# Grouped attention's scores as three products of rounded halves instead of one fp32 product

## The chip, the cores and the metric

The kernel runs on one core of a Trainium2 chip. The metric is the device time of one execution in microseconds (us); a version's time is the median of three runs. The core's engines that matter here are TensorE (PE: matrix products and transposes, written to PSUM banks of 128 x 512 fp32), ScalarE (ACT), VectorE (DVE), and the queue of SyncE (SP), which starts most of the loads.

## The reference, cut to what matters

The reference is two transformer-like blocks of two layers each over 512 tokens of width 2048, all in fp32. The change touches one of the three attention branches of the first block, branch A (grouped attention, 8 query heads over 2 key heads, 128 wide):

```
proj = rms_norm(x, g_pre) @ w_in            # 2048 -> 5952, split into a_q, a_k, a_v, a_g, ...
qa = rope_axial(rms_norm(a_q), row, col)    # 512 tokens x 8 heads x 128
ka = rope_axial(rms_norm(a_k), row, col)    # 512 tokens x 2 heads x 128
s  = einsum('bqkgd,bskd->bkgqs', qa, ka) * 128 ** -0.5      # all 512 keys, no mask
p  = softmax(s)
o_a = (p @ va) * silu(a_g)
...
y = concat(o_a, o_b, o_c) @ w_out
x = x + rms_norm(y, g_post)
```

## The kernel before, in words

**Panels.** All large products (`panel`, L619 to L643) run as "panels" of 512 output columns. Each weight tile arrives in `stage`; ScalarE writes its rounded copy `whi` (type F32R), VectorE writes the rest `wlo = stage - whi`, and TensorE adds up three products of rounded operands: `hi_x*lo_w`, `hi_x*hi_w`, `lo_x*hi_w` (L635, L636, L637). The activations are split the same way into `act_hi` and `act_lo`. The product of the two low parts is left out.

**Branch A.** After panel 8 of each of the first block's two layers, the branch starts. Queries and keys lie in `zone` with tokens on the partitions. A "turn job" (`job`, L668) transposes one head's four 128 x 128 tiles into one of two banks `JOB`; VectorE copies the bank to `zone` (`take_job`, L1473) as `kT_a` (2 heads) or `qT_a` (ring of 4 heads). Two key jobs and the first query job come first, and then one query job per head, one head ahead of its use.

Scores go by "units": unit i is head i // 4 and query tile i % 4, 32 units per layer. TensorE's order for unit i is: `score(i)`, one fp32 product of 128 x 128 with 128 x 512 (L680); `turn(i-2)`, four transposes of the probabilities (L689); `pv(i-3)`, four fp32 products with the values (L698). At i = 0, 4, 8, ... the next head's query job (L668) stands in front.

- VectorE for unit i: `row_max(i)`, a maximum over 512 scores (L1489) and its product with a scale (L1491); then `finish(i-3)`, a reciprocal and two products (L1501, L1503, L1506). At a head's first unit, the copy of the next head's queries (L1473) stands in front.
- ScalarE for unit i: `take_turn(i-2)`, copying turned probabilities out of their bank (L1152); then `exp(i)` (L1144).

Each engine executes its own list in order, and semaphores tie them. `score(i)` waits for `exp(i-2)`, since it writes the bank that this one reads; `turn(i)` waits for `exp(i)`; `pv(i)` waits for `take_turn(i)` and for `finish(i-2)`. A query job waits until the job two before it has left its bank (`job_ev`), and a head's first score waits for `job_ev` of its queries. No scheduler is at work: the order is that of the loops.

Of the kernel before, what the change touches and what calls it, by code (L numbers as in the profile page):

```python
# [8 lines left out]
F32 = mybir.dt.float32  # L9
F32R = mybir.dt.float32r  # L10
I32 = mybir.dt.int32
ALU = mybir.AluOpType
ACT = mybir.ActivationFunctionType
AX = mybir.AxisListType

P = 128
SEQ = 512
TT = SEQ // P
# [10 lines left out]
HD = 128  # L29
A_H, A_KV, B_H, C_H = 8, 2, 4, 4  # L30
# [104 lines left out]
def build(nc, io, only_first=False):  # L135


    with ExitStack() as ctx:
# [26 lines left out]
        zone_at = place[0]  # L165
# [45 lines left out]
        def view(first, *shape, of=zone):  # L211

            size = int(np.prod(shape))
            names = "abcd"[:len(shape)]
            v = of[:, first:first + size]
            if len(shape) == 1:
                return v
            return v.rearrange(f"p ({' '.join(names)}) -> p {' '.join(names)}",
                               **{n: s for n, s in zip(names, shape)})

        xs = view(0, TT, DM)
        probs = view(PP, 4, SEQ)
        probsT = view(PP + 2048, 4, SEQ)
        tanh_tmp = view(ZT, 2, PW)
# [22 lines left out]
        def count(name, per1, per2=None, credit=0):  # L247
            return Count(sem(name), (per1, per1 if per2 is None else per2), credit)
# [18 lines left out]
        J1, J2 = 46, 29  # L267
        job_done = count("job_done", J1, J2)
        job_ev = count("job_ev", J1, J2, credit=2)
        score_done = count("score_done", UNITS, PAIRS)  # L270
        max_done = count("max_done", UNITS, 2 * PAIRS)
        exp_done = count("exp_done", UNITS, PAIRS, credit=2)
# [62 lines left out]
        qT_c, kT_c, v_c = view(ZT, C_H, SEQ), view(ZK, C_H, SEQ), view(ZV, TT, PW)  # L335
        g_c = view(ZQ, C_H, GM, GRID_W)
        q_a, kv_a = view(ZQ, TT, A_H * HD), view(ZV, TT, 2 * A_KV * HD)
        qT_a, kT_a = view(ZT, 4, SEQ), view(ZK, A_KV, SEQ)

        cq_b, ckv_b = view(ZQ, TT, B_Q), view(ZV, TT, B_CKV_W)  # L340
        wuq, wukv = view(PP, 4, 768), view(ZK, 2, 1024)
# [15 lines left out]
        def tok(t):  # L357
            return slice(t * P, (t + 1) * P)
# [2 lines left out]
            return [(qT_c[:, h, tok(t)], kT_c[:, h, :])]  # L361

        def scores_a(h, t):
            return [(qT_a[:, h % 4, tok(t)], kT_a[:, h // 4, :])]

        def scores_b(h, t):
            return [(qnT[:, h, tok(t)], knT[:, h, :]), (qpT[0:B_ROPE, h, tok(t)], kpT[0:B_ROPE, :])]
# [10 lines left out]
        def turn_job(srcs, width, dst, scale=1.0):  # L378
            return ("turn", srcs, width, dst, scale)

        def mm_job(groups, n, dst, scale=1.0):
# [3 lines left out]
                  for h in range(C_H)] + \  # L385
                 [turn_job([view(PP, TT, PW)[:, t, h * HD:(h + 1) * HD] for t in range(TT)], P, qT_c[:, h, :], -SC_C)
                  for h in range(C_H)]
        JOBS_AK = [turn_job([kv_a[:, t, h * HD:(h + 1) * HD] for t in range(TT)], P, kT_a[:, h, :]) for h in range(A_KV)]
        JOBS_AQ = [turn_job([q_a[:, t, h * HD:(h + 1) * HD] for t in range(TT)], P, qT_a[:, h % 4, :]) for h in range(A_H)]
        B_QC, B_KC = KC, KC + 4  # L390
        wuq_h = wuq.rearrange("p k (h e) -> p k h e", h=B_H)
        wukv_h = wukv.rearrange("p k (h e) -> p k h e", h=B_H)
# [624 lines left out]
        def _(act):  # L1017
# [129 lines left out]
            def take_turn(blk, l, br, i):  # L1147
                u = br["first"] + i
                act.wait_ge(turn_done.sem, turn_done.at(blk, l, u + 1))
                act.wait_ge(pv_done.sem, pv_done.at(blk, l, u + 1 - 4))  # L1150
                w = P * len(range(TT))
                act.activation(probsT[:, u % 4, 0:w], TURN[u % 2][:, 0:w], ACT.Copy).then_inc(pt_done.sem, 1)  # L1152

            def attention(blk, l, br):
                n = 4 * br["heads"]
                for i in range(n + 2):
                    if i >= 2:
                        take_turn(blk, l, br, i - 2)
                    if i < n:
                        exp(blk, l, br, i)  # L1160

            def pair_exp(l, i):
                w = P * len(keys_of(i % 4))
# [39 lines left out]
            with act.Fori(0, 2) as l:  # L1203
                for j in range(LEAD):
                    split_hi(0, l, 0, j)
                act.wait_ge(job_ev.sem, job_ev.at(0, l, 1))
                in_panel(l, 0, take_copy(lambda t, p: view(0, TT, PW)[:, t, :]), turned=turned_then_saved(l),
                         between=squares_between(l))
                in_panel(l, 1, take_copy(lambda t, p: view(2048, TT, PW)[:, t, :]), row=0)
                in_panel(l, 2, take_copy(lambda t, p: v_c[:, t, :]), row=1)  # L1210
                in_panel(l, 3, take_tanh(), row=2)
                attention(0, l, BR_C)
                with act.Fori(4, 6) as p:
                    in_panel(l, p, take_copy(lambda t, p: zone[:, bass.ds(ZQ + t * 1024 + (p - 4) * PW, PW)]), row=p - 1)
                in_panel(l, 6, take_copy(lambda t, p: kv_a[:, t, :]), row=5)
                in_panel(l, 7, take_tanh(), row=6)
                in_panel(l, 8, take_tanh())
                attention(0, l, BR_A)
                in_panel(l, 9, take_copy(lambda t, p: cq_b[:, t, :]), next_width=B_CKV_W)
                in_panel(l, 10, take_copy(lambda t, p: ckv_b[:, t, :], B_CKV_W), width=B_CKV_W, row=7)  # L1220
                in_panel(l, 11, take_tanh(), row=8)
                attention(0, l, BR_B)
                out_panel(0, l, NIN, True, turned=turned_hi(0, l, KC, 0.5))
                out_panel(0, l, NIN + 1, True)
                out_panel(0, l, NIN + 2, True, row=9)
                out_panel(0, l, NP - 1, False, row=10)
                mod_row_out(l, NIN - 1)
# [71 lines left out]
            with act.Fori(0, 2) as l:  # L1299
# [21 lines left out]
                high = turned_hi(1, l, KC, 0.5)  # L1321
# [17 lines left out]
        def _(dve):  # L1339
# [125 lines left out]
            def take_job(blk, l, n, jb):  # L1465
# [8 lines left out]
                else:  # L1474
                    dve.tensor_scalar(dst, src, scale, None, ALU.mult).then_inc(job_ev.sem, 1)

            def row_max(blk, l, br, i):
                u = br["first"] + i
                h, t = i // 4, i % 4
                dve.wait_ge(score_done.sem, score_done.at(blk, l, u + 1))  # L1480


                s, m, nm = SCORE[u % 2][:, :], nmx[:, u % 4, 0:1], nmx[:, u % 4, 1:2]
                if br["name"] == "C":
                    bias = g_c[:, h, 6 - 2 * t:14 - 2 * t, :].rearrange("p m k -> p (m k)")
                    apart(dve)
                    dve.tensor_tensor_reduce(s, s, bias, 1.0, 3.0e38, ALU.add, ALU.min, nm).then_inc(max_done.sem, 1)
                elif br["name"] == "A":
                    dve.tensor_reduce(m, s, AX.X, ALU.max, negate=True).then_inc(dve_link.next(), 1)  # L1489
                    dve.wait_ge(dve_link.sem, dve_link.now(blk, l))  # L1490
                    dve.tensor_tensor(nm, m, rsq[:, t, h:h + 1], ALU.mult).then_inc(max_done.sem, 1)  # L1491
                else:
                    dve.tensor_reduce(nm, s, AX.X, ALU.max, negate=True).then_inc(max_done.sem, 1)  # L1493
# [178 lines left out]
            for l in range(2):  # L1672
# [24 lines left out]
                panel(0, l, 6, take_copy(lambda t, p: kv_a[:, t, :]), mod=6)  # L1697
                panel(0, l, 7, take_gate(lambda p: 0, lambda p: 1), between=a_between1(l))
                panel(0, l, 8, take_gate(lambda p: PW, lambda p: 2), between=a_between2(l))
                j0 = BR_A["j0"]  # L1700
                for n, jb in enumerate(JOBS_AK + JOBS_AQ[0:1]):
                    take_job(0, l, j0 + n, jb)

                def next_queries(h):
                    if h + 1 < A_H:
                        take_job(0, l, j0 + 3 + h, JOBS_AQ[h + 1])
                attention(0, l, BR_A, next_queries)
                panel(0, l, 9, take_copy(lambda t, p: cq_b[:, t, :]), next_width=B_CKV_W, mod=7)
                panel(0, l, 10, take_copy(lambda t, p: ckv_b[:, t, :], B_CKV_W), width=B_CKV_W, mod=8)
# [465 lines left out]
```

## Time and profile before

| what | value |
|---|---|
| median of 3 runs | 3671.71 us (3661.34 to 3674.33) |
| the profiled execution's own time, core 0 | 3671.2 us, its span from first to last instruction 3671.2 us |
| PE busy | 3515.5 us, 96% |
| DVE busy | 1834.7 us, 50% |
| ACT busy | 1113.0 us, 30% |
| mean granted clock of TensorE | 0.979 |
| branch A, layer 0 (first transpose to next panel) | 481.17 to 558.92 us |

An engine's busy time is a share of the whole span. Matmuls are pipelined and the printed length of one is modelled, so the pace of TensorE is read from the distance between starts. A printed fp32 product of 512 columns has two records, and an fp32 product of 128 columns also has two.

### The profile page before, as it was taken

What the parts mean: (1) busy time and instruction counts of PE and PEld (TensorE: products, weight loads), DVE (VectorE), ACT (ScalarE), POOL (GpSimd) and SP (SyncE); (2) the same over time, 40 slices, a digit from 0 to 9 for tenths busy, and PEclk for the clock granted to TensorE, in tenths of its full rate; (3) what the DMA queues carried; (4) which work ended last, traced back from release to release, by engine and by line L of the source; (5) the groups of instructions that cost most, each with busy time, mean ns of one, the idle gap of its engine ahead of it and who ended that gap; (6) DMA issues with size and microseconds to landing.
All of it is one profiled execution on the core that took longest, in us unless ns stands there. A gap on an engine that the chain in (4) does not pass through costs nothing.

```text
span 3671.2 us, 49811 instructions
## 1 busy us (share of the span) xinstructions
PE 3515.5 (96%) x17037; PEld 2800.2 (76%) x17037; DVE 1834.7 (50%) x3318; ACT 1113.0 (30%) x1784; POOL 151.9 (4%) x218
## 2 busy tenths in 40 slices
PE   7999999999999999999997999999997999999998
PEld 6878878668787887875876887787786888778786
DVE  5555765445665556654456323546625332626543
ACT  3232242132322323422223223432323222522431
POOL 1101001001110100000010000000000000000000
PEclk9999999999999999999998999999998999999999
DMA  7636316025664452330644332231333333033142
GB/s 267 209 94 198 112 30 204 29 103 179 203 210 148 156 159 60 115 118 1 207 149 136 92 100 66 61 103 36 134 100 113 98 97 97 18 95 92 53 149 97
DMA packets 183839, 430.27 MB, mean 117 GB/s; under 512 B 18166, under 2 KB 25777, under 8 KB 177240
## 3 DMA queue, kind: packets, MB, share of 16 engines
q1 hardware_dynamic: 151144, 298.11, 25.4%
q0 software_dynamic: 28992, 104.43, 9.2%
q10 hardware_dynamic: 3504, 25.22, 1.7%
q8 instruction: 108, 1.77, 0.2%
q14 instruction: 91, 0.75, 0.1%
HBM read 406.61 MB, written 24.75 MB: 117 GB/s over the span
## 4 chain that ended last, share of the span: by engine, by line
PE 89%; DVE 6%; DMA 2%; issue 2%; ACT 1%; DVEq 0%; ACTq 0%; SPq 0%; POOLq 0%
PE bank L635 23%; PE bank L637 23%; PE bank L636 23%; PE bank L680 4%; PE bank L698 3%; PE bank L672 2%; PE bank L689 2%; PE bank L659 1%; PE bank L835 1%; PE bank L813 1%; DMA wmod<-in_w_mod 1%; PE bank L824 1%; PE bank L668 1%; PE bank L889 1%; PE bank L876 1%
## 5 line engine op out<-in xcount | busy, mean ns | idle before, releaser
L635 PE MATMUL bank<-wlo,act_hi 128*128 128x512 f32 (+1 forms) x3968 | 1552.3, 391 | 9.2 <-DVE zone L1394 4.6
L637 PE MATMUL bank<-whi,act_lo 128*128 128x512 f32 (+1 forms) x3968 | 1538.5, 388 | 0.0
L636 PE MATMUL bank<-whi,act_hi 128*128 128x512 f32 (+1 forms) x3968 | 1538.2, 388 | 0.0
L1347 DVE TENSOR_TENSOR wlo<-stage,whi 128x1024 fp32r<-128x1024 f32 (+1 forms) x496 | 598.1, 1210 | 810.6 <-ACT whi L1023 809.0
L1023 ACT ACTIVATE whi<-stage 128x1024 fp32r<-128x1024 f32 (+1 forms) x496 | 514.8, 1048 | 1469.0 <-PE bank L637 816.8
L635 PEld LDWEIGHTS bank<-wlo,act_hi 128*128 128x128 f32 x3968 | 747.3, 188 | 181.1 <-issue 21.2
L637 PEld LDWEIGHTS bank<-whi,act_lo 128*128 128x128 f32 x3968 | 747.1, 188 | 152.7
L636 PEld LDWEIGHTS bank<-whi,act_hi 128*128 128x128 f32 x3968 | 747.7, 188 | 146.5
L1362 DVE SCALAR_TENSOR_TENSOR macc<-wmod,csil,macc 128x512 f32<-128x512 f32 x360 | 269.8, 749 | 101.5 <-DMA wmod<-in_w_mod 72.2
L2130 POOL DMA_DIRECT2D wmod<-in_w_mod x192 | 136.6, 712 | 1749.6 <-DVE macc L1362 1728.6
L1152 ACT ACTIVATE zone<-bank 128x512 f32<-128x512 f32 x128 | 76.4, 597 | 137.2 <-PE bank L689 137.0
L689 PEld LDWEIGHTS bank<-ident,zone 128*128 128x128 f32 x512 | 61.4, 141 | 67.6 <-issue 61.7
L1523 DVE TENSOR_TENSOR Y<-bank,zone 128x512 f32<-128x512 f32 (+1 forms) x64 | 43.2, 691 | 123.2 <-ACT mprod L1191 65.6
L680 PE MATMUL bank<-zone 128*128 128x512 f32 x192 | 98.7, 599 | 5.7 <-ACT zone L1144 3.9
L698 PE MATMUL bank<-zone 128*128 128x128 f32 x768 | 101.0, 275 | 0.0
L1412 DVE SCALAR_TENSOR_TENSOR Y<-zone,bank 128x512 f32<-128x512 f32 (+1 forms) x64 | 43.6, 687 | 104.9 <-ACT zone L1073 102.9
L698 PEld LDWEIGHTS bank<-zone 128*128 128x128 f32 x768 | 93.2, 192 | 0.0
L659 PE MATMUL bank<-ident,Y 128*128 128x128 f32 x384 | 59.6, 289 | 27.5 <-DMA Y<-in_x 14.1
L1144 ACT ACTIVATE zone<-bank,nmx 128x512 f32<-128x512 f32 x64 | 43.8, 685 | 125.0 <-DVE nmx L1493 104.1
L659 PEld LDWEIGHTS bank<-ident,Y 128*128 128x128 f32 x384 | 49.1, 149 | 39.7 <-issue 21.5
L689 PE MATMUL bank<-ident,zone 128*128 128x128 f32 x512 | 78.4, 276 | 0.0
L680 PE MATMUL bank<-late 64*128 64x512 f32 (+1 forms) x128 | 66.8, 622 | 1.6 <-DVE late L1473 1.6
(222 smaller groups left out, 2465.3 us busy)
## 6 DMA issues: line engine op xcount, KB each, us to landing
stage<-in_w_in SPq DMA_DIRECT2D x352, 512.0 KB, 3.7
wmod<-in_w_mod POOLq DMA_DIRECT2D x192, 512.0 KB, 4.4
stage<-in_w_out SPq DMA_DIRECT2D x128, 512.0 KB, 3.9
out<-Y ACTq DMA_DIRECT2D x20, 1024.0 KB, 5.5
zone<-out SPq DMA_DIRECT2D x4, 4096.0 KB, 15.3
stage<-in_w_in SPq DMA_DIRECT2D x16, 320.0 KB, 3.8
Y<-in_x ACTq DMA_DIRECT2D x4, 1024.0 KB, 9.1
rpb_tiles<-rpb_pad POOLq DMA_DIRECT2D x16, 224.0 KB, 7.6
```

What stands on the lines that cost most here:

```text
L635: pe.matmul(out, hi_x, lo_w, start=(k == 0), stop=False)
L636: pe.matmul(out, hi_x, hi_w, start=False, stop=False)
L637: mm = pe.matmul(out, lo_x, hi_w, start=False, stop=(k == KC - 1))
L659: tr = pe.transpose(XP[k % 4][:, tok(t)], src[:, t, tok(k)], ident[:, :])
L680: mm = pe.matmul(SCORE[u % 2][:, 0:P * len(range(TT))], lhs, rhs, start=(r == 0), stop=(r == len(parts) - 1))
L689: mm = pe.transpose(TURN[u % 2][:, tok(kt)], probs[:, u % 4, tok(kt)], ident[:, :])
L698: mm = pe.matmul(OUTB[u % 2][:, 0:HD], probsT[:, u % 4, tok(n)], br["v"](i // 4, kt), start=(n == 0), stop=(n == len(tiles) - 1))
L1023: act.activation(whi[:, j % RH, :, 0:width], stage[:, j % RS, :, 0:width], ACT.Copy)\
L1152: act.activation(probsT[:, u % 4, 0:w], TURN[u % 2][:, 0:w], ACT.Copy).then_inc(pt_done.sem, 1)
L1347: dve.tensor_tensor(wlo[:, j % RH, :, 0:width], stage[:, j % RS, :, 0:width], whi[:, j % RH, :, 0:width].bitcast(F32), ALU.subtract).then_ ...
L1362: dve.scalar_tensor_tensor(out=macc[:, :], in0=wmod[:, i % 2, k % 2, :], scalar=csil[:, k:k + 1], in1=macc[:, :], op0=ALU.mult, op1=ALU.ad ...
L2130: pool.dma_start(wmod[:, i % 2, :, :], src.rearrange("o (a p) n -> p (o a) n", p=P))\
```

## The change

Queries and keys of branch A are kept as two F32R tiles, high and low. `split_a` holds 4 x 2 x 512 columns, in the place of the old `qT_a` and `kT_a` and of what was free behind them; the ring of queries goes from 4 heads to 2. A job's bank is now read twice: ScalarE copies it with rounding to the high part (`split_high`), and VectorE, once that is there, subtracts the high part from the bank (`split_low`). `job_ev` comes from `split_low`. A score is three F32R products into the same bank instead of one fp32 product; the product of the two low parts is left out.

```diff
+        split_a = sb("split_a", [P, 4, 2, SEQ], F32R, at=zone_at + 4 * ZT)
+        a_hi = count("a_hi", A_KV + A_H, 0)
...
-        qT_a, kT_a = view(ZT, 4, SEQ), view(ZK, A_KV, SEQ)
+        qT_hl, kT_hl = split_a[:, 0:2, :, :], split_a[:, 2:4, :, :]
...
         def scores_a(h, t):
-            return [(qT_a[:, h % 4, tok(t)], kT_a[:, h // 4, :])]
+            q, k = qT_hl[:, h % 2, :, :], kT_hl[:, h // 4, :, :]
+            return [(q[:, 1, tok(t)], k[:, 0, :]), (q[:, 0, tok(t)], k[:, 1, :]), (q[:, 0, tok(t)], k[:, 0, :])]
...
+        SPLIT_A = [kT_hl[:, h, :, :] for h in range(A_KV)] + [qT_hl[:, h % 2, :, :] for h in range(A_H)]
...                                                     # ScalarE
-            def attention(blk, l, br):
+            def attention(blk, l, br, early=None):
                 n = 4 * br["heads"]
                 for i in range(n + 2):
                     if i >= 2:
                         take_turn(blk, l, br, i - 2)
+                    if early and i % 4 == 0 and i < n:
+                        early(i // 4)
                     if i < n:
                         exp(blk, l, br, i)
+
+            def split_high(l, m):
+                n = BR_A["j0"] + m
+                act.wait_ge(job_done.sem, job_done.at(0, l, n + 1))
+                act.activation(SPLIT_A[m][:, 0, :], JOB[n % 2][:, :], ACT.Copy).then_inc(a_hi.sem, 1)
...
-                attention(0, l, BR_A)
+                for m in range(A_KV + 1):
+                    split_high(l, m)
+                attention(0, l, BR_A, lambda h: split_high(l, A_KV + 1 + h) if h + 1 < A_H else None)
...                                                     # VectorE
+            def split_low(l, m):
+                n = BR_A["j0"] + m
+                dve.wait_ge(a_hi.sem, a_hi.at(0, l, m + 1))
+                high, low = SPLIT_A[m][:, 0, :], SPLIT_A[m][:, 1, :]
+                dve.tensor_tensor(low, JOB[n % 2][:, :], high.bitcast(F32), ALU.subtract).then_inc(job_ev.sem, 1)
...
-                j0 = BR_A["j0"]
-                for n, jb in enumerate(JOBS_AK + JOBS_AQ[0:1]):
-                    take_job(0, l, j0 + n, jb)
+                for m in range(A_KV + 1):
+                    split_low(l, m)
 
                 def next_queries(h):
                     if h + 1 < A_H:
-                        take_job(0, l, j0 + 3 + h, JOBS_AQ[h + 1])
+                        split_low(l, A_KV + 1 + h)
```

TensorE's list at the start of head 1 (unit 4) before: a query job, then `score(4)` into bank4, `turn(2)` into bank2, `pv(1)` into bank7.

```order
L668 MATMUL bank1<-ident_60,zone_56 128x128 x4
L767 REGISTER_ALU
L677 REGISTER_ALU
L680 MATMUL bank4<-zone_56 128x512
L689 MATMUL bank2<-ident_60,zone_56 128x128 x4
L698 MATMUL bank7<-zone_56 128x128 x4
```

The same place in the changed kernel (its lines stand 4 further down).

```order
L672 MATMUL bank1<-ident_60,zone_56 128x128 x4
L771 REGISTER_ALU
L681 REGISTER_ALU
L684 MATMUL bank4<-split_a_93 128x512 x3
L693 MATMUL bank2<-ident_60,zone_56 128x128 x4
L702 MATMUL bank7<-zone_56 128x128 x4
```

Nothing moved on TensorE: one product became three in the same place.

ScalarE's list there before: `exp(3)`, `take_turn(2)` from bank2, `exp(4)`, `take_turn(3)`, `exp(5)`.

```order
L1144 ACTIVATE zone_56,sm_74<-bank5,nmx_73,rsq_72 128x512
L1149 REGISTER_ALU
L1152 ACTIVATE zone_56<-bank2 128x512
L1144 ACTIVATE zone_56,sm_74<-bank4,nmx_73,rsq_72 128x512
L1149 REGISTER_ALU
L1152 ACTIVATE zone_56<-bank3 128x512
L1144 ACTIVATE zone_56,sm_74<-bank5,nmx_73,rsq_72 128x512
```

And in the changed kernel:

```order
L1148 ACTIVATE zone_56,sm_74<-bank5,nmx_73,rsq_72 128x512
L1153 REGISTER_ALU
L1156 ACTIVATE zone_56<-bank2 128x512
L1171 REGISTER_ALU
L1172 ACTIVATE split_a_93<-bank1 128x512
L1148 ACTIVATE zone_56,sm_74<-bank4,nmx_73,rsq_72 128x512
L1153 REGISTER_ALU
L1156 ACTIVATE zone_56<-bank3 128x512
L1148 ACTIVATE zone_56,sm_74<-bank5,nmx_73,rsq_72 128x512
```

The split (L1172) is new; it stands behind the copy of the turned probabilities of two units before and ahead of the head's first exp. On VectorE the copy of the queries, L1473, is replaced one for one by the subtraction, L1496, ahead of the head's first row maximum:

```order
L1496 TENSOR_TENSOR split_a_93<-bank1,split_a_93 128x512
L1510 TENSOR_REDUCE nmx_73<-bank4 128x1
L1512 TENSOR_TENSOR nmx_73<-nmx_73,rsq_72 128x1
L1522 RECIPROCAL ri_75<-sm_74 128x1
L1524 TENSOR_TENSOR ri_75<-ri_75,xr_64 128x1
```

Its number of instructions is unchanged; what it waits for is now ScalarE and no longer TensorE.

## Rows read from the trace of the kernel before

**Rows 1.** The page: busy time of each engine, then the chain of waits by line.

```profile
PE 3515.5 (96%) x17037; PEld 2800.2 (76%) x17037; DVE 1834.7 (50%) x3318; ACT 1113.0 (30%) x1784; POOL 151.9 (4%) x218
PE bank L635 23%; PE bank L637 23%; PE bank L636 23%; PE bank L680 4%; PE bank L698 3%; PE bank L672 2%; PE bank L689 2%; PE bank L659 1%; PE bank L835 1%; PE bank L813 1%; DMA wmod<-in_w_mod 1%; PE bank L824 1%; PE bank L668 1%; PE bank L889 1%; PE bank L876 1%
```

**Rows 2.** Busy time by stretch, branch A of layer 0: stretch, length, engines, clock, DMA.

```profile
481.40:484.80 3.40, 3.38 (x16) 2.56 (x14) 2.07 (x3) 0.00 (x0) 0.00 (x0) 0.50 0.00 0
484.80:491.20 6.40, 5.38 (x24) 2.99 (x23) 4.07 (x9) 3.49 (x8) 0.00 (x0) 1.00 0.00 0
486.50:556.50 70.00, 68.98 (x448) 52.86 (x448) 49.51 (x157) 42.85 (x95) 0.00 (x0) 1.00 0.01 1
```

**Rows 3.** Timeline of one head of branch A: start, length, engine, line, operation.

```profile
500.62 0.60 PE L668 MATMUL bank<-ident,zone 128*128 128x128 f32 x4
501.06 1.02 PE L680 MATMUL bank<-zone 128*128 128x512 f32 x2
501.92 0.60 PE L689 MATMUL bank<-ident,zone 128*128 128x128 f32 x4
502.12 0.69 DVE L1489 TENSOR_REDUCE nmx<-bank 128x1 f32<-128x512 f32 x1
502.36 1.06 PE L698 MATMUL bank<-zone 128*128 128x128 f32 x8
502.56 0.60 ACT L1152 ACTIVATE zone<-bank 128x512 f32<-128x512 f32 x1 [1.27 <-PE bank L689]
502.85 0.16 DVE L1491 TENSOR_TENSOR nmx<-nmx,rsq 128x1 f32<-128x1 f32 x1
503.05 0.77 ACT L1144 ACTIVATE zone<-bank,nmx,rsq 128x512 f32<-128x512 f32 x1
503.25 1.02 PE L680 MATMUL bank<-zone 128*128 128x512 f32 x2
...
509.82 0.60 PE L668 MATMUL bank<-ident,zone 128*128 128x128 f32 x4
```

**Rows 4.** Timeline of the start of branch A, layer 0.

```profile
481.17 3.72 PE L668 MATMUL bank<-ident,zone 128*128 128x128 f32 x16 [2.13 <-DVE Y L1412]
482.12 0.69 DVE L1473 COPY zone<-bank 128x512 f32<-128x512 f32 x1 [1.49 <-PE bank L668]
...
484.08 0.69 DVE L1473 COPY zone<-bank 128x512 f32<-128x512 f32 x1 [0.42 <-PE bank L668]
484.83 1.98 PE L680 MATMUL bank<-zone 128*128 128x512 f32 x4
...
486.91 0.78 ACT L1144 ACTIVATE zone<-bank,nmx,rsq 128x512 f32<-128x512 f32 x1 [7.00 <-DVE nmx L1491]
487.83 1.13 PE L680 MATMUL bank<-zone 128*128 128x512 f32 x2 [1.02 <-ACT zone L1144]
```

**Rows 5.** Timeline: three rounded products per group; first among fp32 transposes, then alone.

```profile
28.30 0.60 PE L659 MATMUL bank<-ident,Y 128*128 128x128 f32 x4
28.66 0.48 PE L635 MATMUL bank<-wlo,act_hi 128*128 128x512 f32 x1
28.97 0.39 PE L636 MATMUL bank<-whi,act_hi 128*128 128x512 f32 x1
...
31.50 0.60 PE L659 MATMUL bank<-ident,Y 128*128 128x128 f32 x4
...
463.69 0.39 PE L637 MATMUL bank<-whi,act_lo 128*128 128x512 f32 x1
...
478.65 0.39 PE L637 MATMUL bank<-whi,act_lo 128*128 128x512 f32 x1
```

**Rows 6.** Splits elsewhere in the kernel, by line: count, shortest/median/longest in ns.

```profile
L1101 ACT ACTIVATE act_hi<-bank x64: 578/598/622, 788.1 to 3508.8; 128x512 fp32r<-128x512 f32 x64
L1461 DVE TENSOR_TENSOR act_lo<-zone,act_hi x32: 691/693/694, 1955.5 to 2856.9; 128x512 fp32r<-128x512 f32 x32
```

More of the change, by code:

```diff
@@ L387, in build @@
                   for h in range(C_H)]
-        JOBS_AK = [turn_job([kv_a[:, t, h * HD:(h + 1) * HD] for t in range(TT)], P, kT_a[:, h, :]) for h in range(A_KV)]
-        JOBS_AQ = [turn_job([q_a[:, t, h * HD:(h + 1) * HD] for t in range(TT)], P, qT_a[:, h % 4, :]) for h in range(A_H)]
+        JOBS_AK = [turn_job([kv_a[:, t, h * HD:(h + 1) * HD] for t in range(TT)], P, None) for h in range(A_KV)]
+        JOBS_AQ = [turn_job([q_a[:, t, h * HD:(h + 1) * HD] for t in range(TT)], P, None) for h in range(A_H)]
+        SPLIT_A = [kT_hl[:, h, :, :] for h in range(A_KV)] + [qT_hl[:, h % 2, :, :] for h in range(A_H)]
         B_QC, B_KC = KC, KC + 4
```

## The prediction

> **What bounds the kernel now.** I read the page first: busy shares, then the chain of waits by line [rows 1]. TensorE is busy 96% of the span, and the chain is nearly all TensorE: the reader should see that 69% of it is the three panel lines and only 4% the line of the fp32 scores, L680, which branch A shares with two other branches. So the change can touch a few per cent of the time at most. Next the busy table by stretch: in branch A of layer 0 TensorE works 68.98 of 70.00 us at full clock, VectorE 49.51 and ScalarE 42.85 [rows 2]. TensorE bounds the branch, the other two have slack on average. Last the timeline of one head, which gives every step [rows 3]. From start to start: four transposes 0.44 us (500.62 to 501.06), a score 0.86 (to 501.92), transposes 0.44 (to 502.36), the value products 0.89 (to 503.25). A unit is 2.19, and a head with its query job 0.44 + 4 x 2.19 = 9.20, which is 500.62 to 509.82. There is no idle time in it.
>
> **The score itself.** The fp32 product (0.86) becomes three rounded ones. The panels run that shape: 22 groups of three lie between 463.69 and 478.65, so a group takes 14.96 / 22 = 0.68 [rows 5]. A unit saves 0.18 and takes 2.01. What lies beside TensorE allows this: over 32 units VectorE's busy time is 49.51 / 32 = 1.55 a unit and ScalarE's 42.85 / 32 = 1.34 [rows 2]; both are below 2.01.
>
> Three rounded products between fp32 transposes might pay for the switch. The panel with transposes says how much: the first product of a group holds its place for 0.31 (28.66 to 28.97), 0.08 more than the usual 0.23, but the four transposes before it hold theirs for only 0.36, 0.08 less than 0.44. The whole round, 12 products and 4 transposes, is 3.20 (28.30 to 31.50); 12 x 0.227 + 0.44 is 3.16 [rows 5]. So I take no cost per switch; the bounds are 0 and 0.08 a unit.
>
> The trace has 0.86 for the fp32 product and 0.68 for three rounded ones, so the saving is a fifth. The Trainium skill (FP8 and Floating Point Precision, TensorE Precision Notes) says that true fp32 goes through the array in four passes; three passes would then take 0.645, an estimate by that page, a unit would save 0.215, and the same sum as below would end at +2.6 us and not at +4.4. The measured row decides.
>
> **The start of the branch.** Before, three jobs go through two banks, each emptied by one VectorE copy: the first bank is ready at 482.12, the third at 484.08, and the first score starts 0.75 after that [rows 4]. Now each bank needs ScalarE's rounding copy, 0.60 [rows 6] and 0.04 of hand-over (the product at 502.85 lasts 0.16 and its reader starts at 503.05 [rows 3]), and then VectorE's subtraction, 0.69 [rows 6], in place of a copy of 0.69 [rows 4]. The third job waits for the first bank: 0.64 later. Its own bank takes 0.64 longer too. The first score starts 1.28 later, about 486.1. From there to the third score the chain is score, maximum, exp, 3.00 from 484.83 to 487.83 [rows 4], now 0.18 shorter. So the third score starts 1.10 later than before. The fourth bank's split (the next head's queries) fits in front of the first maximum: its rounding copy is done while the first score runs.
>
> **The start of each later head.** This is where a wait is added. VectorE's subtraction waits for ScalarE's rounding copy; that stands behind `take_turn` of two units before; and queued behind the subtraction is the row maximum of the head's first unit u. Who waits for it: exp(u), and then score(u+2), which needs the bank. From the query job's first transpose, with durations of rows 3:
>
> - 0.44 job; 0.68 score(u); turn(u-2) starts at 1.12;
> - its reader starts 0.64 after a turn does (501.92 to 502.56): `take_turn` at 1.76, done at 2.36;
> - rounding copy 0.60 and hand-over 0.04: subtraction at 3.00, done at 3.69;
> - maximum to exp 0.93 (502.12 to 503.05): exp(u) at 4.62;
> - exp to the score two later 0.92 (486.91 to 487.83 [rows 4]): score(u+2) at 5.54.
>
> TensorE itself would be there at 0.44 + 2 x 2.01 = 4.46. It stands idle for 1.08. In the kernel before, the copy needs only the transposes, is over before score(u) ends, and costs nothing. A head is now 0.44 + 4 x 2.01 + 1.08 = 9.56 instead of 9.20: the stall eats the 0.72 saved and 0.36 more. After the stall the three engines are in step again before the next head begins. There are six such heads a layer (1 to 6): head 0's wait lies in the start, and head 7 has no successor to prepare. The stall's bounds: 0, if the list's slack is greater than I read it; 1.25, if the rounding copy takes as long as the exp that reads a bank of the same size, 0.77 and not 0.60 [rows 3].
>
> **The sum.** Per layer: +1.10 at the third score, 30 units after it at -0.18, that is -5.40, and 6 stalls of 1.08, that is +6.48; together +2.18. Branch A runs in two layers: +4.4 us. Nothing else moves: the panel after the branch starts when TensorE arrives, no DMA is added, and SyncE's load of the next branch's weights waits for the end of branch A as before. The profiled execution is 3671.2 us and its span the same, the median 3671.71, so I add to either and get 3675.6 to 3676.1. I take 3676.
>
> **Rivals.**
>
> *The stall is hidden (faster).* If the boundary chain has slack, only the start is paid: 2 x (1.10 - 5.40) = -8.6, about 3663. For it: VectorE and ScalarE are at 71% and 61% in the branch [rows 2]. Against it: these are averages; the four links between the turn and the exp are in series, and by the rows they add to a time 1.08 past the point where TensorE arrives. This is also the most that the change can win, short of 2 x 5.76 = 11.5 with a free start.
>
> *The clock falls (slower).* TensorE's clock was 0.50, its level of 1.2 GHz, from 481.40 to 484.80, after an idle time of 2.13 before 481.17 [rows 2, 4]. If each new stall brought such a stretch, TensorE would lose half of 3.4, 1.7 us, twelve times: 20.4 more, 3696. It decides when at least 8 of the 12 stalls do it (14 us, with the 4.4). Against it: in 484.80:491.20 TensorE idles for 1.02 just before 487.83 and the clock reads 1.00 [rows 2, 4]; a stall of 1.08 in 9.56 is of that size. The Trainium skill (TensorE: Matmul & The Clock Gate, A second HAM failure mode: psum-queue depth-cycling) describes a kernel whose frequent short idle times between groups of products made the clock swing between its levels; that speaks for this rival, while this trace shows the opposite for one such stall.
>
> *The switch between fp32 and rounded products costs* its 0.08 in each unit: +5 us, 3681. For it: the slot of 0.31. Against it: the round of 3.20, which contains the switch both ways.
>
> *The products aren't what they say:* three at the fp32 pace would be 3 x 0.86, 1.72 more for each of 64 units, 3786. Against it: the type is that of `whi` and `act_hi`, whose pace is 0.68 for three.
>
> **Chances.** Forecast 0.65; stall hidden 0.11; clock 0.05; switch 0.15; wrong pace 0.01; the rest is unknown, on both sides. About 0.5% (18 us) is what a measurement of this kernel can tell from no change. Forecast, hidden stall and switch all lie within it: same 0.93. Slower takes the clock and the wrong pace, less the cases where only some stalls bring the clock down: 0.05. Faster needs more than the 11.5 us that are there to win: 0.02. The range holds the forecast with its bounds (stalls of 0 to 1.25, switch of 0 to 0.08) and the spread of the median of three, whose runs before lie between 3661 and 3674: 3663 to 3685.
>
> **What would show it.** In the profile after: three products per score, start to start 0.68 to the transposes behind them; a unit of 2.01 inside a head; idle time of about 1.1 before the third score of heads 1 to 6, put down to exp; VectorE's subtraction waiting about 2 us for ScalarE's split; a head of 9.5 to 9.6; the first score some 1.3 later after the first transpose; granted clock 1.00 from the first scores to the branch's end. Heads of 8.5 would prove the first rival right, a clock under 0.9 in the branch the second, units of 2.09 the third. The prediction is wrong if the heads 1 to 6, which took 9.20 before, come out below 9.3 or above 9.8.

## The result, and the profile after

The changed kernel takes 3674.87 us (median of 20 runs, 3669.38 to 3682.37), the kernel before 3670.36 (20 runs beside them). The ratio is 1.0020, 95% interval 1.0013 to 1.0027: slower, by 4.5 us between the medians and 7.3 by the ratio (4.8 to 9.9 by its interval). The forecast was 3676 and 4.4 us. The profiled execution took 3680.51 us, with a span of 3678.8.

The page after, in the rows that answer to [rows 1]:

```profile
span 3678.8 us, 49979 instructions
PE 3511.7 (95%) x17101; PEld 2815.1 (77%) x17101; DVE 1829.6 (50%) x3318; ACT 1124.5 (31%) x1804; POOL 151.8 (4%) x218
PE bank L639 22%; PE bank L641 22%; PE bank L640 22%; PE bank L684 4%; PE bank L702 3%; PE bank L676 2%; PE bank L693 2%; PE bank L839 1%; PE bank L663 1%; PE bank L817 1%; DMA wmod<-in_w_mod 1%; PE bank L828 1%; PE bank L672 1%; PE bank L893 1%; PE bank L880 1%
```

TensorE has 64 more matmul records (three per score where there were two), is busy 3.8 us less, and the span is 7.6 longer. So TensorE's idle time grew by 11.4 us. The timeline of head 2 in branch A of layer 0 shows where (the columns are start, length, engine, line, operation, and the idle time before it with its releaser; rows of other instructions in between are left out here and in the timelines below):

```profile
504.30 0.60 PE L672 MATMUL bank<-ident,zone 128*128 128x128 f32 x4
504.65 0.93 PE L684 MATMUL bank<-split_a 128*128 128x512 f32 x3
505.42 0.60 PE L693 MATMUL bank<-ident,zone 128*128 128x128 f32 x4
506.06 0.60 ACT L1156 ACTIVATE zone<-bank 128x512 f32<-128x512 f32 x1 [1.10 <-PE bank L693]
506.55 0.59 ACT L1172 ACTIVATE split_a<-bank 128x512 fp32r<-128x512 f32 x1
506.67 0.94 PE L684 MATMUL bank<-split_a 128*128 128x512 f32 x3
507.18 0.69 DVE L1496 TENSOR_TENSOR split_a<-bank,split_a 128x512 fp32r<-128x512 f32 x1 [1.94 <-ACT split_a L1172]
507.79 0.68 DVE L1510 TENSOR_REDUCE nmx<-bank 128x1 f32<-128x512 f32 x1
508.69 0.78 ACT L1148 ACTIVATE zone<-bank,nmx,rsq 128x512 f32<-128x512 f32 x1 [1.55 <-DVE nmx L1512]
509.62 0.98 PE L684 MATMUL bank<-split_a 128*128 128x512 f32 x3 [0.68 <-ACT zone L1148]
511.68 0.94 PE L684 MATMUL bank<-split_a 128*128 128x512 f32 x3
```

Against [rows 3]: the scores start at 504.65, 506.67, 509.62 and 511.68. A plain unit is 2.02 (was 2.19), but the one before the head's third score is 2.95. The chain in between is the forecast one, link by link: `take_turn`, rounding copy, subtraction, maximum, exp, score. VectorE stood idle for 1.94 ahead of the subtraction. The waits between 496 and 552 us, by who waited for whom (total, times, longest), say that this happens at all six heads:

```profile
DVE split_a L1496 <- ACT split_a L1172: 11.6, 6, 1.9
ACT zone L1148 <- DVE nmx L1512: 9.3, 6, 1.6
PE bank L684 <- ACT zone L1148: 4.1, 6, 0.7
```

From job to job, heads 1 to 5 take 9.47 (9.46 to 9.49) in both layers, against 9.20 before and 9.56 forecast; head 6 has the same late third score.

The second surprise is in the start. The busy table by stretch, where [rows 2] had one stretch of 3.4 us at clock 0.50 (columns: stretch, length, PE, PEld, DVE, ACT, POOL, granted clock, DMA share, GB/s):

```profile
480.70:494.30 13.60, 11.79 (x40) 8.98 (x41) 6.17 (x12) 6.00 (x13) 0.00 (x0) 0.50 0.00 0
1443.30:1450.10 6.80, 5.47 (x18) 3.68 (x16) 3.61 (x6) 2.60 (x5) 0.00 (x0) 0.50 0.00 1
496.00:552.00 56.00, 51.94 (x380) 46.68 (x379) 37.05 (x124) 35.97 (x77) 0.00 (x0) 1.00 0.01 1
```

In layer 0 TensorE ran at 0.50, its level of 1.2 GHz, for 13.6 us, through all four jobs and the first scores; in layer 1 for 6.8. With the stalls, from 496 to 552, it is at 1.00. The start itself, to be read against [rows 4]:

```profile
480.60 1.83 PE L672 MATMUL bank<-ident,zone 128*128 128x128 f32 x8 [2.13 <-DVE Y L1426]
481.61 0.60 ACT L1172 ACTIVATE split_a<-bank 128x512 fp32r<-128x512 f32 x1 [2.28 <-PE bank L672]
482.24 0.69 DVE L1496 TENSOR_TENSOR split_a<-bank,split_a 128x512 fp32r<-128x512 f32 x1 [2.19 <-ACT split_a L1172]
483.08 1.94 PE L672 MATMUL bank<-ident,zone 128*128 128x128 f32 x8 [0.65 <-DVE split_a L1496]
485.58 2.93 PE L684 MATMUL bank<-split_a 128*128 128x512 f32 x6 [0.56 <-DVE split_a L1496]
489.11 1.65 PE L684 MATMUL bank<-split_a 128*128 128x512 f32 x3 [0.60 <-ACT zone L1148]
```

The first score comes 4.98 after the first transpose (3.65 before). From the first transpose to the next panel's first product, the whole branch takes 82.75 in layer 0 and 80.01 in layer 1; before, 77.74 and 77.77. These 7.2 us are nearly the 7.6 between the spans of the two profiled executions, but other stages differ too (one takes 2.2 us more, others less) and happen nearly to cancel.

### The profile page after: what moved, and what is told of

It is laid out like the page before. It is cut to its first block, busy times and chain, and to the rows that moved or that the text cites. A ratio compares the mean times of both kernels' runs of the same rounds, so it can differ in the third digit from the quotient of the medians.

```text
span 3678.8 us, 49979 instructions
## 1 busy us (share of the span) xinstructions
PE 3511.7 (95%) x17101; PEld 2815.1 (77%) x17101; DVE 1829.6 (50%) x3318; ACT 1124.5 (31%) x1804; POOL 151.8 (4%) x218
## 3 DMA queue, kind: packets, MB, share of 16 engines
q8 instruction: 107, 1.75, 0.2%
## 4 chain that ended last, share of the span: by engine, by line
PE 86%; DVE 7%; DMA 3%; issue 2%; ACT 1%; DVEq 0%; ACTq 0%; SPq 0%; POOLq 0%
PE bank L639 22%; PE bank L641 22%; PE bank L640 22%; PE bank L684 4%; PE bank L702 3%; PE bank L676 2%; PE bank L693 2%; PE bank L839 1%; PE bank L663 1%; PE bank L817 1%; DMA wmod<-in_w_mod 1%; PE bank L828 1%; PE bank L672 1%; PE bank L893 1%; PE bank L880 1%
## 5 line engine op out<-in xcount | busy, mean ns | idle before, releaser
L684 PE MATMUL bank<-split_a 128*128 128x512 f32 x192 | 63.8, 445 | 10.5 <-ACT zone L1148 9.3
```

The costliest lines, as they stand in the source:

```text
L684: mm = pe.matmul(SCORE[u % 2][:, 0:P * len(range(TT))], lhs, rhs, start=(r == 0), stop=(r == len(parts) - 1))
```

## The experiments

All compare with runs of the kernel before on the same chip. "Branch" is branch A from first transpose to the next panel, in layers 0 and 1.

| kernel | median us (runs) | before beside it | ratio, 95% interval | branch, layers 0 and 1 | us at clock 0.50 in its start |
|---|---|---|---|---|---|
| kernel before | 3670.36 (20) | | | 77.74, 77.77 | 3.4, 3.4 |
| change, first set | 3674.87 (20) | 3670.36 | 1.0020, 1.0013 to 1.0027 | 82.75, 80.01 | 13.7, 6.8 |
| `again` | 3675.83 (12) | 3669.74 | 1.0017, 1.0006 to 1.0029 | 82.72, 82.71 | 13.7, 13.7 |
| `e1_split_first` | 3663.94 (12) | 3669.74 | 0.9989, 0.9979 to 0.9999 | 76.93, 76.95 | 13.7, 13.7 |
| `e2_wait_alone` | 3684.40 (6) | 3669.74 | 1.0051, 1.0034 to 1.0067 | 84.33, 85.40 | 6.8, 10.2 |
| `e3_two_jobs` | 3663.07 (12) | 3669.74 | 0.9985, 0.9974 to 0.9995 | 74.60, 73.87 | 6.8, 3.4 |
| `e4_one_product` | 3641.49 (4) | 3668.34 | 0.9934, 0.9917 to 0.9951 | 64.44, 65.12 | 10.2, 10.2 |
| `e5_fill_gap` | 3658.08 (8) | 3668.34 | 0.9970, 0.9960 to 0.9980 | 73.72, 73.70 | 0, 0 |
| `e6_fill_gap_in_change` | 3667.49 (12) | 3668.34 | 1.0000, 0.9991 to 1.0009 | 80.97, 78.76 | 6.8, 0 |
| `e7_fill_all` | 3662.48 (12) | 3668.34 | 0.9983, 0.9974 to 0.9992 | 73.66, 73.65 | 0, 0 |
| `e8_fill_three` | 3656.63 (12) | 3667.61 | 0.9973, 0.9960 to 0.9985 | 74.32, 73.72 | 3.4, 0 |
| `e9_fill_before` | 3665.32 (11) | 3667.61 | 0.9993, 0.9982 to 1.0005 | 77.00, 77.01 | 0, 0 |

**The changed kernel again** (`again`), nothing altered.

> The changed kernel once more, nothing altered, for a second trace. Its first trace has heads 1 to 6 of branch A at 9.47 us in both layers, but the stretch from the branch's first transpose to the next panel took 82.75 us in layer 0 and 80.01 in layer 1, where the kernel before takes 77.74 and 77.77. The granted clock was 0.50 for 13.65 us at the start of layer 0's branch and for 6.83 in layer 1, against 3.41 in both layers before. Theory (the work costs 2.2 us a layer, the rest is the clock's chance): heads 9.47 again, and a stretch between 79.9 and 80.2 where the clock is low for up to 6.8 us, longer where it is low for longer. Rival (layer 0 has a cause of its own, a wait that layer 1 lacks): 82.7 again in layer 0 whatever the clock. Time 3675, 4 to 7 above before.

Measured: heads of 9.47 to 9.49 again, and now layer 1 too has the long stretch and the long branch:

```profile
479.90:493.50 13.60, 11.79 (x40) 8.98 (x40) 6.17 (x12) 6.08 (x13) 0.00 (x0) 0.50 0.00 0
1439.10:1452.70 13.60, 11.79 (x40) 8.98 (x39) 6.17 (x12) 6.07 (x13) 0.00 (x0) 0.50 0.00 1
```

The rival falls: layer 1 can do what layer 0 did. Three of four traced branches have 13.7 us at 0.50 and last 82.7; the fourth has 6.8 and lasts 80.0.

**The split first in ScalarE's list** (`e1_split_first`).

```diff
                 for i in range(n + 2):
+                    if early and i % 4 == 0 and i < n:
+                        early(i // 4)
                     if i >= 2:
                         take_turn(blk, l, br, i - 2)
-                    if early and i % 4 == 0 and i < n:
-                        early(i // 4)
                     if i < n:
                         exp(blk, l, br, i)
```

> The changed kernel with one swap on ScalarE: at a head's first unit the rounding copy stands ahead of the copy of the turned probabilities, no longer behind it. Theory (the stall of 1 us before a head's third score comes from this place in ScalarE's list): the split can start 0.64 after the job does, VectorE's subtraction ends near 2.0, the first maximum starts then and the third score is released near 3.85, ahead of TensorE's 4.46; heads 1 to 6 take 0.44 + 4 x 2.02 = 8.52 instead of 9.47, 12 heads save 11 us: 3664, 6 to 7 below the kernel before. Rival (the stall comes from VectorE, which has a subtraction of 0.69 more to wait for, or from the rounded products): heads stay near 9.47 and the time near 3675.

Measured: heads of 8.51 and 8.52, time 3663.94. In the timeline the split runs while TensorE is at the head's first score, and the third score is not late:

```profile
501.61 0.60 PE L672 MATMUL bank<-ident,zone 128*128 128x128 f32 x4
502.25 0.60 ACT L1172 ACTIVATE split_a<-bank 128x512 fp32r<-128x512 f32 x1
502.88 0.69 DVE L1496 TENSOR_TENSOR split_a<-bank,split_a 128x512 fp32r<-128x512 f32 x1 [0.32 <-ACT split_a L1172]
503.49 0.68 DVE L1510 TENSOR_REDUCE nmx<-bank 128x1 f32<-128x512 f32 x1
504.40 0.78 ACT L1148 ACTIVATE zone<-bank,nmx,rsq 128x512 f32<-128x512 f32 x1 [0.43 <-DVE nmx L1512]
506.01 0.93 PE L684 MATMUL bank<-split_a 128*128 128x512 f32 x3
```

VectorE waits 0.32 for the split, not 1.94, and the exp ends near 505.2, well ahead of 506.01. Two lines changed place, nothing else, and 12 us went: the stall is shown to come from the place in ScalarE's list. This version is faster than the kernel before, although both its starts had 13.7 us at 0.50.

**The wait without the rounded products** (`e2_wait_alone`), an edit to the kernel before.

```diff
+            def spare_copy(l, m):                       # ScalarE, called where the change calls split_high
+                n = BR_A["j0"] + m
+                act.wait_ge(job_done.sem, job_done.at(0, l, n + 1))
+                act.activation(view(ZK + 1024, 2, SEQ)[:, m % 2, :], JOB[n % 2][:, :], ACT.Copy).then_inc(a_hi.sem, 1)
...
                     if h + 1 < A_H:                     # VectorE
+                        dve.wait_ge(a_hi.sem, a_hi.at(0, l, 4 + h))
                         take_job(0, l, j0 + 3 + h, JOBS_AQ[h + 1])
```

> The kernel before with the chain of the split and nothing else of the change: ScalarE copies each job's bank to an unused place of the same size, at the place in its list where the change has the rounding copy, and VectorE's old copy waits for it. Scores stay fp32 products. Theory (the wait alone makes the stall): from the job's start 0.44 + 0.86, reader of the turn at 1.94, ScalarE's copy to 2.54, VectorE's copy 3.18 to 3.87, exp at 4.80, third score at 5.72 less the 0.08 by which the measured chain was shorter, against TensorE's 4.82; heads 9.20 + 0.82 = 10.02, 12 heads 9.8 us and the two starts 2.4: 12 above before, 3682. Rival (the stall belongs to the three rounded products): heads stay 9.20, time within 3 us of before.

Measured: heads of 9.97, so 0.77 for the stall, and 14.7 us more in all. The waits from 496 to 552 us have the same three links as in the changed kernel:

```profile
DVE zone L1483 <- ACT zone L1168: 12.6, 6, 2.1
ACT zone L1145 <- DVE nmx L1501: 9.3, 6, 1.6
PE bank L681 <- ACT zone L1145: 3.1, 6, 0.5
```

So the wait makes the stall with fp32 scores too, and the rounded products are not its cause. (The three copies at the branch's start wait in the same way; those lines are left out above.) The start again took more than the 1.2 expected a layer. Its work is that of the kernel before and its chain is longer, and the low stretches went from 3.4 to 6.8 and 10.2.

**Two jobs at the start** (`e3_two_jobs`), an edit to `e1_split_first`.

```diff
+        KQ_A = JOBS_AK[0:1] + JOBS_AQ[0:3] + JOBS_AK[1:2] + JOBS_AQ[3:]      # SPLIT_A in the same order
+        AT_UNIT = {1: 2, 4: 3, 6: 4, 8: 5, 12: 6, 16: 7, 20: 8, 24: 9}       # unit: job that stands before it
+        READY_A = [2, 3, 4, 6, 7, 8, 9, 10]                                  # head: jobs that must be split
...
-                for n, jb in enumerate(JOBS_AK + JOBS_AQ[0:1]):
-                    job(0, l, j0 + n, jb)
+                for m in range(2):
+                    job(0, l, j0 + m, KQ_A[m])
```

> The kernel of the swap, with a shorter start besides: only the first key head and the first query head are turned and split before the first score; the second query head's job moves to unit 1 and the second key head's job to unit 6 (it is first needed by head 4). Theory (the start costs 1.1 us a layer because a third bank must go through both splits): first score about 3.3 after the first transpose instead of 4.98 and 4.63, heads 2 to 6 at 8.52 and head 1 one job longer, 0.44; about 1.3 a layer below the swap alone: 3661. Rival (the start is bounded by something else, as the clock): first score no earlier than 4.5, time equal to the swap alone.

Measured: the first score 2.91 and 2.64 after the first transpose, head 1 at 8.95, heads 2 to 6 at 8.51. The branch is 2.3 and 3.1 shorter than in `e1_split_first`, more than the 1.3 expected; the low stretches are shorter as well. In the time of whole runs the gain over `e1_split_first` is only 0.9 us and lies inside the intervals.

**One product per score** (`e4_one_product`), an edit to `e1_split_first`; the two products with a low part are left out.

```diff
-            return [(q[:, 1, tok(t)], k[:, 0, :]), (q[:, 0, tok(t)], k[:, 1, :]), (q[:, 0, tok(t)], k[:, 0, :])]
+            return [(q[:, 0, tok(t)], k[:, 0, :])]
```

> The kernel of the swap with one product per score, high times high; the two products with a low part are left out (so the low parts are made and not read). It asks what bounds a unit once the score is short. Theory (TensorE still bounds it, VectorE and ScalarE just below): unit 0.44 + 0.89 + 0.23 = 1.56, VectorE needs 0.86 for the maximum with its scale and 0.67 for the finish, 1.53 in all; heads 6.7, and 64 units save 0.45 against the swap's 2.02: 3635. Rival (VectorE's printed lengths and hand-overs count in full, 0.89 + 0.74 + 0.14 = 1.77, so that it takes over): unit 1.77, heads 7.5, time 3648.

Measured: 3641.49 and heads of 7.26, between the two. The timeline has both reasons:

```profile
501.64 0.50 PE L684 MATMUL bank<-split_a 128*128 128x512 f32 x1 [0.31 <-ACT zone L1148]
503.22 0.48 PE L684 MATMUL bank<-split_a 128*128 128x512 f32 x1
504.87 0.60 PE L672 MATMUL bank<-ident,zone 128*128 128x128 f32 x4
505.07 0.78 ACT L1148 ACTIVATE zone<-bank,nmx,rsq 128x512 f32<-128x512 f32 x1
505.22 0.48 PE L684 MATMUL bank<-split_a 128*128 128x512 f32 x1
505.85 0.58 ACT L1172 ACTIVATE split_a<-bank 128x512 fp32r<-128x512 f32 x1
506.46 0.69 DVE L1496 TENSOR_TENSOR split_a<-bank,split_a 128x512 fp32r<-128x512 f32 x1 [0.65 <-ACT split_a L1172]
506.79 0.48 PE L684 MATMUL bank<-split_a 128*128 128x512 f32 x1
508.90 0.50 PE L684 MATMUL bank<-split_a 128*128 128x512 f32 x1 [0.31 <-ACT zone L1148]
```

A plain unit is 1.58 (501.64 to 503.22), as the theory said, and VectorE, whose rival figure was 1.77, keeps up. But the unit before a head's third score is 2.11 (506.79 to 508.90). With TensorE that much shorter, the split is late again even from its better place: the job starts at 504.87, ScalarE is still busy until 505.85 with the exp of the unit before, and the subtraction starts at 506.46. The expectation missed that.

**The filled gap** (`e5_fill_gap`), an edit to `e3_two_jobs`.

```diff
                 panel(0, l, 8)
+                for _ in range(16):
+                    pe.transpose(SCORE[0][:, 0:P], ident[:, :], ident[:, :])
                 banks_free(l, 9)
```

> The kernel with two jobs at the start, and 16 transposes of the identity, written to a bank that nothing reads, in the 2.1 us in which TensorE waits for VectorE between panel 8 and the first job. They add 1.8 us of work where TensorE is idle and touch nothing else. Theory (the stretch at clock 0.50 follows the idle time before the first job, and doubles the first jobs and scores): the clock stays at 1.00 through the jobs, the first score comes 2.5 instead of 2.9 and 2.6 after the first transpose, and each branch is 1 to 3 us shorter: 3660, 3 below the kernel with two jobs. Rival (the clock falls with the gaps of the job stage itself, whatever came before): the same 3.4 to 13.7 us at 0.50, no gain.

Measured: no low stretch in either start, first score 2.64 in both layers, branches of 73.72 and 73.70, time 3658.08. The clock's column in the start of both branches:

```profile
480.90:490.90 10.00, 6.14 (x36) 4.67 (x37) 4.93 (x10) 4.70 (x11) 0.00 (x0) 1.00 0.00 0
1430.00:1440.00 10.00, 6.14 (x36) 4.68 (x37) 4.94 (x10) 4.71 (x11) 0.00 (x0) 1.00 0.00 1
```

TensorE is busy for only 6.14 of these 10 us, with idle times of up to 1.57, and stays at 1.00. So here it was the gap ahead of the start that mattered. The first score came about as expected, but the branches are only 0.88 and 0.17 shorter than in `e3_two_jobs`, not 1 to 3, so they don't account for the 5 us between the medians. By ratio this is the fastest version that keeps the three products, 0.3% below the kernel before, and its interval lies below the changed kernel's.

**The same filling in the changed kernel** (`e6_fill_gap_in_change`) and **in the kernel before** (`e9_fill_before`); the edit is the one above.

> The changed kernel with the same 16 transposes in the gap ahead of the first job and nothing else. Both traces of the changed kernel have 82.7 us per branch where the clock is at 0.50 for 13.65 us and 80.0 where it is for 6.83. Theory (the gap starts the low stretch): clock 1.00 or a short stretch, branch at 79 to 80 in both layers, 3670. Rival (the idle times of the longer start, 0.65 before the third job, 0.56 before the first score and 0.60 before the third, keep it low by themselves): 13.65 again somewhere, branch 82, time 3675.

> The kernel before with the 16 transposes in the gap ahead of branch A and nothing of the change. It asks how much of the gain of the kernel with two jobs and filled gap is the clock's, for both score forms. Theory: before, one stretch of 3.4 us at 0.50 covers the four jobs of the start; without it the branch is 76.7 instead of 77.75, 2 us in all: 3667, so that rounded scores are worth 3.0 us a branch (76.7 against 73.7) when nothing stalls. Rival (the filling costs what it gives, or the low stretch comes anyway): 77.7 and no change of time.

Measured: the changed kernel with filling is level with the kernel before (ratio 1.0000). In layer 1 it has no low stretch. In layer 0 one of 6.8 us comes later, at 483.6, after the first jobs. So a filled gap doesn't rule the low stretch out, and the rival holds a part. That it is the start's own idle times that bring it is not shown: in layer 1 the same start, with the same waits, kept 1.00. Its start in layer 1, TensorE alone:

```profile
1436.03 1.06 PE L672 MATMUL bank<-ident,zone 128*128 128x128 f32 x8 [0.38 <-issue]
1438.16 1.22 PE L672 MATMUL bank<-ident,zone 128*128 128x128 f32 x8 [1.07 <-DVE split_a L1498]
1440.21 1.65 PE L684 MATMUL bank<-split_a 128*128 128x512 f32 x6 [0.82 <-DVE split_a L1498]
1443.05 0.96 PE L684 MATMUL bank<-split_a 128*128 128x512 f32 x3 [1.19 <-ACT zone L1150]
```

The start of the kernel before with filling, layer 0:

```profile
478.93 1.07 PE L668 MATMUL bank<-ident,zone 128*128 128x128 f32 x8 [0.38 <-issue]
480.43 1.23 PE L668 MATMUL bank<-ident,zone 128*128 128x128 f32 x8 [0.44 <-DVE zone L1475]
481.84 1.98 PE L680 MATMUL bank<-zone 128*128 128x512 f32 x4 [0.18 <-DVE zone L1475]
484.85 1.13 PE L680 MATMUL bank<-zone 128*128 128x512 f32 x2 [1.02 <-ACT zone L1146]
```

These are the two starts at full clock. The third score comes 7.02 after the first transpose in one and 5.92 in the other: 1.10 apart. The branches are 78.76 and 77.01, 1.75 apart: that is the change without the clock. For the kernel before, filling shortens the branch by 0.75, less than the 1.05 expected, and the gain in time, 0.9993 with an interval over 1, is not shown. From its 77.0 to the 73.7 of `e5_fill_gap` are 3.3 us a branch (3.0 expected): what rounded scores give at full clock, with no stall and two jobs at the start.

**More filling** (`e7_fill_all`, `e8_fill_three`), edits to `e5_fill_gap`: 12 and 10 more transposes inside the start (all to a value bank, `OUTB[0]`), and the same 16 ahead of branches C and B.

> As the kernel with two jobs and the filled gap, with 12 more transposes of the identity between the second job and the first score and 10 before the third score, where TensorE waits 1.4 and 1.1 us. Theory (idle time anywhere in the start lets the clock fall): clock 1.00 through the whole start, branch 72.5 to 73 instead of 73.9 and 74.6, 3659. Rival (the fillings delay the real work more than the clock gives back, since 12 of them are 1.3 us at full clock and 2.6 at half): first score later than 2.9, branch 75 or more.

> The kernel with two jobs and the filled gap, with the same 16 transposes of the identity also in the like gaps ahead of the first block's two other branches, C (2.5 us near 209) and B (2.4 us near 683). Theory (a low stretch follows such a gap and doubles the first jobs of the branch): the stretches at 0.50 that began at 211.7 and 686.2 before get shorter or go, up to 1.7 us for C and up to 5 us for B in each layer where TensorE is busy in them, in all 2 to 8 us: 3653. Rival (in these branches TensorE waits for VectorE's bank copies anyway, so the clock doesn't bound the job stage): lows gone, time within 2 us of 3658.

Measured: with the inner filling the branch is 73.66 and 73.65, no shorter than 73.7, since the clock was at 1.00 already; the median is 3662.48, not below 3658.08. Branch A doesn't explain these 4 us, but they go with the clock of the whole execution. Its 12 runs have a mean granted clock of 0.9793, the 8 of `e5_fill_gap` 0.9808, and within these runs the time rises by 2.7 us for each 0.001 of clock lost. That leaves 0.2 us, plus or minus 2.0 (an estimate; each run's clock is on record to 0.001). With filling ahead of all three branches, branch C of layer 0 goes from 43.87 to 42.94 and B from 102.22 to 101.60, but one start of A had a low stretch of 3.4 again (74.32); the ratio of 0.9973 can't be told from 0.9970, and the 5 us expected are not shown. Nor is it shown that the filling did it: without any filling there, C took 42.94 in `e7_fill_all` and B 101.61 in `e3_two_jobs`.

## Why the prediction was right

**The size and the sign** came out: 3674.87 against 3676, inside the range, and slower by less than 0.5%. That the difference of medians (4.5) so nearly equals the sum (4.4) is luck: two errors of opposite sign meet in it, the work costs less than forecast (3.5) and the clock takes more, and by the ratio the loss is 7.3, with the 4.4 just below its interval.

**TensorE bounds the branch, and a unit shrinks to 2.01:** 2.02 measured in all plain units. The rival with a cost per switch between fp32 and rounded products (2.09) is out. The Trainium skill's four passes (FP8 and Floating Point Precision, TensorE Precision Notes) would have given an estimate of 0.645 for the three products and a unit of 1.98; the trace has 0.69, from 2.02 less 0.44 and 0.89. One sign came out otherwise: from a score to the transposes behind it are 0.77 (504.65 to 505.42) and not 0.68, and from the value products to the next score 0.81 (505.86 to 506.67) and not 0.89. It is the shift of 0.08 that the prediction read in the panel, and it cancels in the unit.

**The stall** is where it was forecast, at the third score of heads 1 to 6, and by the links forecast. It is 0.93 (2.95 less 2.02) and not 1.08. The links are 0.22 shorter by the head's rows: 506.06 to 506.55 is 0.49, where the sum had 0.60; 507.18 to 507.79 is 0.61, where it had 0.69; 507.79 to 508.69 is 0.90, where it had 0.93. In the first two an instruction that waits for nothing starts before the printed end of the one ahead of it on its engine, and the sum took the printed lengths. The other 0.07 goes on TensorE's side: the first score starts 0.35 after the job and not 0.44, so TensorE is there at 4.39 (504.30 to 504.65, and twice 2.02) and not at 4.46. The rival with a hidden stall is refuted by the trace, and `e1_split_first` shows what it would have been worth: 12 us, not the 13 of the sum.

**The start** was forecast 1.10 later at the third score. At full clock it is 1.10 (`e6_fill_gap_in_change` against `e9_fill_before`). In the traces of the change itself it is 1.85 and 1.47, 8.51 and 8.15 after the first transpose against 6.66 and 6.68.

**The step that failed** is the sentence in the prediction's last part that the granted clock would be 1.00 from the first scores to the branch's end. The clock rival was looked for in the six stalls, where it didn't come: 1.00 from 496 to 552 us, in six stalls of 0.93. It came in the start, which the sum took over with the old stretch of 3.4 us: the low stretch lasted 13.7 us in three branches of four and 6.8 in the fourth. A branch of the change is 78.76 without a low stretch (`e6_fill_gap_in_change`, layer 1), 80.0 to 81.0 with 6.8 us and 82.7 with 13.7. So the clock takes up to 4.0 us of a branch, where it took 0.75 before; the difference, up to 3.2, is more than the 1.75 of the work. `e2_wait_alone` shows that the start's longer chain goes with longer stretches, for it adds only the copies and the wait (6.8 and 10.2 against 3.4 and 3.4, two branches of each). Which part of the chain does it stays open: TensorE is now idle for 0.65 before the third job and 0.56 before the first score, where it wasn't, but for 0.60 before the third score, where it was idle for 1.02 [rows 4], and no run fills these idle times without the gap ahead. The Trainium skill (TensorE: Matmul & The Clock Gate, A second HAM failure mode: psum-queue depth-cycling) says that frequent short idle times let the clock swing. In the heads the trace contradicts it, with 1.00 through six idle times of 0.7; in the start the trace has one long low stretch and not a swing.

**The sum without the clock** is 1.10, less 30 x 0.17, plus 6 x 0.93, that is 1.58 a layer; 1.75 was measured at full clock, 2.18 forecast. With it the change would cost 3.5 us. Set against the kernel before as it is, the traced branches give 7.2 and, by the second trace, 9.9 us. The medians differ by only 4.5 and 6.1, and both traces are of executions that took longer than the median: 3680.51 against 3674.87, and 3686.22, the longest of its 12. The spread of one kernel's runs, 13 us and more, goes with the clock of the whole execution. Over the 29 runs of the kernel before beside `again`, time and mean granted clock have a correlation of -0.91. The change's 12 runs average 0.9785 and 6.4 us more, these 29 average 0.9798. With 2.4 us for each 0.001, fitted within the two sets, 3.1 of the 6.4 us go with the clock and 3.3 are left, plus or minus 1.3: near the 3.5 of the traces. That is an estimate, and only one pair: `e6_fill_gap_in_change` by the same sum leaves 0.7, plus or minus 1.2.

## What to carry to other kernels

When a copy out of a bank is divided between two engines, look up what stands ahead of the new half in the second engine's list and what is queued behind the old half on the first. Here the saving of 0.17 us in each of 64 units was real and was eaten by 12 waits of 0.93, and moving one call ahead of another turned a loss of 6 us into a gain of 6. Time the start of a stage apart from its steady part, with the granted clock beside it: here the stage started after a gap, and a longer chain in its start also cost clock. And set the mean clock of two versions' runs beside their times before a difference of a few us is put down to the work.

## What the runs showed of the hardware

- In this branch the low stretch at the start follows the idle time ahead of it: all 14 traced starts with the gap of 2.1 us had one, and of 10 with the gap filled only 2 did. 16 transposes that nobody reads, 1.8 us of work in a gap of 2.1, kept the clock at 1.00 through a start in which TensorE was busy for only 6.14 of 10 us (`e5_fill_gap`, both layers). It is no guarantee: the two that had one are layer 0 of `e6_fill_gap_in_change` and of `e8_fill_three`, 4.4 and 2.7 us after the first transpose.
- At the clock's lower level TensorE was busy 11.79 of 13.60 us and did not return to the higher one within them, in the same way in three branches of two executions.
- Three rounded products of 512 columns among fp32 transposes cost no switch in sum: 0.69 a score, against 0.68 in a panel. The score's own place is 0.77, and the fp32 products ahead of it hold theirs for 0.08 less.
- The spread between runs of one kernel goes with the mean granted clock of the execution: 2.3 to 2.5 us for each 0.001 in the three sets of runs of the kernel before, with correlations of -0.89 to -0.95.
